# Filling TensorE's waits with unread products, changing banks and the order of three small steps in a transformer kernel

## The chip, the cores and the metric

The kernel runs on one core of one Trainium2 chip. The metric is the device time of one execution in microseconds (us). Shown is the median of several executions, and beside it one execution that the hardware profiler recorded. All times below are of that one core.

## What is computed

The reference runs two stacks over 256 tokens of width 1024. The first has 16 meta tokens in front (272 columns) and two layers. A layer norms its input, projects it by `w_in`, and feeds four branches: differential attention (a), gated linear attention in two directions (b), latent attention with rotary positions (c), windowed attention (d). Their outputs are projected, gated, summed (`merge`) and projected by `w_out`; then follows a feed-forward part with a convolution of width 3.

```
branches = jnp.stack([o_a, o_b, o_c, o_d], axis=2)
gates = jax.nn.sigmoid(gate_logits.reshape(bsz, T, N_BRANCH, D_MODEL))
merged = jnp.sum(jnp.einsum('btnw,nwd->btnd', branches, w_branch[l]) * gates, axis=2)
h = h + _rms_norm(merged @ w_out[l], norm_mix_post[l])
f = _conv_ffn(_rms_norm(h, norm_ffn_pre[l]), ffn_w_up[l], ...)
```

The second stack has two layers of swiglu, mixer, swiglu over 256 columns; the mixer is a convolution module in its first layer and pooling beside block attention (moba) in its second. A last norm ends it.

## The kernel before, in words

All weights come in slabs of 128 x 1024 numbers through a ring of six buffers (`ring`), in one fixed order, the list `STREAM` (644 slabs). A weight W is split into a rounded part `ring_hi` and a rest `ring_lo`; so is the input (`x_hi`, `x_lo`, or `z_hi`, `z_lo`, or `hid_hi`, `hid_lo`). A product with a slab is then three matmuls for each of eight (or six) blocks k, 24 in all: hi by hi (L403), hi by lo (L404), lo by hi (L405), all into one PSUM bank. `ring_hi` is written by ScalarE (ACT, L958) or, for a third of the `w_in` slabs, by VectorE (DVE, L1700); `ring_lo` by DVE (L1705) or, for some slabs, by GpSimd (POOL, L2488). `low_by(n)` says which.

Each engine has its own program, written out in order by hand, and engines wait for each other by semaphores. Before a bank is written again, TensorE (PE) waits for its last reader; that is `claim(b, *by)`, where `by` names the reader that the next claim will wait for. `begin(name)` waits until the slab's two halves are there. On ACT, `halves(slab)` makes the `ring_hi` of the slab three places further on in the stream, and that needs a free place among four (`HIGH`), so it waits until the slab before `slab` has been used by PE. `low_halves` is the same for `ring_lo` on DVE and POOL. The stream's DMAs are on SP's queue (L2741) and wait for the slab six places back.

Places that matter here:

- `slab_bank` (L289 and following): the bank of a slab. Most take the parity of their place in the stream; the slab (bk, l, 0) has bank 1 and so has (ak, l, 0), two places later. The slabs (mix, 0, 0..3) have banks 4 to 7, and (mix, 0, 4..7) banks 0, 1, 0, 1.
- `first_slab` (L408): the first slab of a part, whose input h is made at the same moment. For each k it has three matmuls (L416, L417, L419) and one of the float32 norm products with `ones` (L423). Its input is made by DVE (L1758, L1760: h; L1693: `z_lo`) and ACT (L997: `z_hi`).
- `norm_gathered` (L456): two norm products at the end of a part (L460, L462). ACT then makes the inverse root `std` (L978, L980).
- `mixers(l)` on PE (L639): among other things it ends with `gate(l, 1, 3)` (a gate is one dense slab), the rotary products (L500), `out_b` of unit 1 (two halves of 3 products of L581 and 8 small products of L586 each) and, for four heads, `scores_c` (L628, L629), gates and so on.
- `mix_out(layer)`: the projection of the second stack's mixer, eight slabs. DVE adds each to h (L1693, h <- bank); ACT makes `z_hi` (L997) and the square (L1485) of it and the next `ring_hi` (L958); DVE makes `z_lo` and the next `ring_lo` (L1705). On ACT the loop is `halves(mix j)`, then `square_x(j)`, which waits for DVE's h of slab j.
- ACT's and DVE's programs for the other parts are unchanged and appear only as the ones that are waited for.

Of the kernel before, what the change touches and what calls it, by code (L numbers as in the profile page):

```python
# [12 lines left out]
P = 128  # L13
KD = D_MODEL // P
# [152 lines left out]
def build(nc, d, out):  # L167
# [4 lines left out]
    with ctx:  # L172
# [13 lines left out]
        cst = sb("cst", N_CST)  # L186
# [104 lines left out]
        def slab_bank(name):  # L291
            if name[0] == "lat":
                return name[2]
            if name[0] in ("up", "gu"):
                n = 2 * name[2] + name[3]
                return n if name[2] < FZ else (n - 2 * FZ) % 4
            if name[0] == "bq" and name[2] == 0:
                return 6
            if name[0] in ("down", "down2"):
                return name[2] % 2  # L300
            if name[0:2] == ("mix", 0) and name[2] < 4:
                return 4 + name[2]
            return N[name] % 2

        def used(name):
# [61 lines left out]
        def tensor_program(pe, c):  # L367
# [3 lines left out]
            def claim(b, *by):  # L371
# [2 lines left out]
                read_by[b] = by  # L374
                return bank[b]

            def begin(name):
                n = N[name]
                assert n == count[0]
                count[0] += 1  # L380
                if STREAM[n][5]:
                    pe.wait_ge(*split(n))
                else:
                    pe.wait_ge(*loaded(n))
                return n % RING, n % HIGH

            def project_raw(name, x, cs, by, ready=None):
                i, _ = begin(name)
                b = claim(slab_bank(name), *by)
                for k in range(KD):  # L390
                    if ready:
                        pe.wait_ge(*at(*ready[k]))
                    m = pe.matmul(b[:, cs], ring[:, i, k * P:(k + 1) * P], x[:, k, cs], start=k == 0, stop=k == KD - 1)  # L393
                m.then_inc(sems["slab_used"], 1)
# [12 lines left out]

            def first_slab(name, b, cs, ready, norm_name, squares, ns):  # L408

                i, i_hi = begin(name)  # L410
                ps = claim(NB, act_, "log", *norm_name)
                for k in range(KD):
                    pe.wait_ge(*at(act_, "z_hi", *ready[k][2:]))
                    c0 = slice(k * P, (k + 1) * P)
                    x1, x2 = z_hi[:, k, cs], z_lo[:, k, cs]
                    pe.matmul(b[:, cs], ring_hi[:, i_hi, c0], x1, start=k == 0, stop=False)  # L416
                    pe.matmul(b[:, cs], ring_lo[:, i, c0], x1, start=False, stop=False)  # L417
                    pe.wait_ge(*at(*ready[k]))
                    m = pe.matmul(b[:, cs], ring_hi[:, i_hi, c0], x2, start=False, stop=k == KD - 1)  # L419
                    if k == KD - 1:  # L420
                        m.then_inc(sems["slab_used"], 1)
                    pe.wait_ge(*at(act_, *squares, k))
                    m = pe.matmul(ps[:, ns], ones, sq[:, k, ns], start=k == 0, stop=k == KD - 1)  # L423
                m.then_inc(*sig(pe_, "norm", *norm_name))
# [1 line left out]
            def project_z(name, cs, by):  # L426
                split_mm(name, claim(slab_bank(name), *by), z_hi, z_lo, 0, KD, cs, True, True)

            def project(name, cs, by, ready=()):
                split_mm(name, claim(slab_bank(name), *by), x_hi, x_lo, 0, KD, cs, True, True, ready)  # L430

            def project_tokens(name, by, tiles):
                i, i_hi = begin(name)
# [19 lines left out]
                    m = pe.matmul(ps[:, cs], ones, sq[:, k, cs], start=i == 0, stop=i == len(squares) - 1)  # L453
                m.then_inc(*sig(pe_, "norm", *name))

            def norm_gathered(name, last, cs=ALL):  # L456

                ps = claim(NB, act_, "log", *name)
                pe.wait_ge(*at(dve_, "gathered", *name))
                pe.matmul(ps[:, cs], ones, sq[:, 0, cs], start=True, stop=False)  # L460
                pe.wait_ge(*at(act_, *last))
                pe.matmul(ps[:, cs], ones, sq[:, KD - 1, cs], start=False, stop=True).then_inc(*sig(pe_, "norm", *name))  # L462
# [107 lines left out]
                                      v_b[r0:r0 + n, t, hh * P:(hh + 1) * P], start=True, stop=True)  # L570
                    m.then_inc(*sig(pe_, "ds", un, w, ch))

            def out_b(un):
                pe.wait_ge(*at(dve_, "state_read", un))
                for hh in range(2):
                    rr = slice(64 * hh, 64 * hh + 64)
                    b = claim(6 + hh, act_, "sqb", un, hh)
                    pe.wait_ge(*at(dve_, "masked", un, hh))
                    for i, t in enumerate((1, 2, 0)):
                        t0, n = TILES[t]  # L580
                        pe.matmul(b[:, t0:t0 + n], v_b[0:n, t, hh * P:(hh + 1) * P], att[0:n, hh, t0:t0 + n], start=i == 0,  # L581
                                  stop=False, skip_group_check=True)
                    todo = [(0, ch) for ch in (1, 2, 3, 4)] + [(1, ch) for ch in (0, 1, 2, 3)]
                    for i, (w, ch) in enumerate(todo):
                        a0, n = CHUNKS[ch][0:2]
                        m = pe.matmul(b[:, a0:a0 + n], state[rr, w, ch, :], q_dec[rr, w, a0:a0 + n], start=False,  # L586
                                      stop=i == len(todo) - 1, skip_group_check=True)
                    m.then_inc(*sig(pe_, "o", un, hh))
# [50 lines left out]
            def mixers(l):  # L639
# [88 lines left out]
                gate(l, 1, 2)  # L728
                latent_q(l, 0)
                latent_v(l, 0)  # L730
                gate(l, 1, 3)
                pe.wait_ge(*at(act_, "kpe", l))
                rope(("K", l), k_pe)
                rope_q(l, 0)
                out_b(B[1])
                for hd in range(4):
                    scores_c(l, hd)
                    first, second = gates_of(hd)
# [35 lines left out]
            def ffn(l):  # L774
                for j in range(KD):
                    b = claim(slab_bank(("out", l, j)), act_, "sqo", l, j)
                    split_mm(("out", l, j), b, z_hi, z_lo, 0, KD, kept(l), True, True,
                             [(dve_, "y_lo", l, k) for k in range(KD)] if j == 0 else ())
                norm_gathered(("out", l), ("sqo", l, KD - 1), kept(l))
                for j in range(NJ):  # L780
                    for gv in range(2):
                        name, by = ("up", l, j, gv), (dve_, "cv3", l, j, gv)
                        if j + gv == 0:
                            first_slab(name, claim(slab_bank(name), *by), kept(l), [(dve_, "z_lo", "ffn", l, k) for k in range(KD)],
                                       ("ffn", l), ("sqf", l), kept(l))
                        elif j < FZ:
                            project_z(name, kept(l), by)
                        else:
                            project(name, kept(l), by, [(dve_, "x_lo", l, k) for k in range(KD)] if (j, gv) == (FZ, 0) else ())
                for j in range(KD):  # L790
                    claim(slab_bank(("down", l, j, 0)), act_, "sqd", l, j)
                    for part, (k0, nk) in enumerate(DOWN):
                        project_down(("down", l, j, part), j, part, fed(l), [(pool_, "hid", l, k0 + k) for k in range(nk)] if j == 0 else ())
                norm_gathered(("down", l), ("sqd", l, KD - 1), fed(l))

            def swiglu(i):
                s = (0, 2, 3, 5)[i]
                for j in range(NJ):
                    for gv in range(2):
# [7 lines left out]
                        elif j < FZ:  # L807
                            project_z(name, SHIFTED, by)
                        else:
                            project(name, TEXT, by, [(dve_, "xs_lo", s, k) for k in range(KD)] if (j, gv) == (FZ, 0) else ())  # L810
                for j in range(KD):
                    claim(slab_bank(("down2", i, j, 0)), dve_, "xd", i, j)
                    for part, (k0, nk) in enumerate(DOWN):
# [15 lines left out]
            def mix_out(layer):  # L829
                whole = range(KD)  # L830
                if layer == 0:
                    for j in range(4):
                        begin(("mix", 0, j))
                        claim(slab_bank(("mix", 0, j)), dve_, "xm", 0, j)
                        mix_part(j, (4, 5, 6), True, False)
                    for j in range(4):
                        mix_part(j, (7,), False, False)
# [2 lines left out]
                    whole = range(4, KD)  # L840
                for j in whole:
                    b = claim(slab_bank(("mix", layer, j)), dve_, "xm", layer, j)
                    split_mm(("mix", layer, j), b, x_hi, x_lo, 0, KD, TEXT, True, True,
                             [(dve_, "y2_lo", layer, k) for k in range(KD)] if j == 0 else ())

# [12 lines left out]
            def conv_mixers():  # L858
# [1 line left out]
                first = [(act_, "xs", 1, k) for k in range(KD)]  # L860
                by = ("a", "a_gate", "cg", "bu", "bg")
                for n, (j, k) in enumerate(CONV_ORDER):
                    project_raw(("conv", j, k) if k < 4 else ("convg", j), u, TEXT, (act_, by[k], j), None if n else first)
                    if (j, k) in ((2, 1), (3, 0), (2, 2), (3, 2)):
                        centred({(2, 1): 0, (3, 0): 1, (2, 2): 2, (3, 2): 3}[j, k])
                    if (j, k) in ((1, 2), (1, 3), (2, 3), (3, 3)):
# [26 lines left out]
                t.then_inc(*sig(pe_, "pv", un, m))  # L893

            def moba():
                project(("moba", 0, 0), TEXT, (act_, "q", ("M", 0, 0)), [(dve_, "xs_lo", 4, k) for k in range(KD)])
                project(("moba", 0, 1), TEXT, (act_, "k", ("M", 0, 0)))
                for i in range(4):
                    project_tokens(("moba", i, 2), (act_, "v", ("M", 0, i)), QT2)
# [34 lines left out]
        def scalar_program(act, c):  # L934
# [598 lines left out]
            def mix_out(layer):  # L1533
# [3 lines left out]
                    for k in range(KD):  # L1537
                        mixed_high(layer, k, *((dve_, "pooled", k) if k < 4 else (act_, "o2", ("M", 0, k - 4), 1)))
                for j in range(KD):
                    if j:  # L1540
                        halves(("mix", layer, j))
                    if j == KD - 1:
                        log_exp_tables()
                    square_x(3 * layer + 2, j, dve_, "xm", layer, j)
# [1384 lines left out]
```

## Time and profile before

| | us |
|---|---|
| three executions | 2355.89, 2352.30, 2357.58 (median 2355.89) |
| the profiled execution, its own time | 2349.86 |
| its span, first to last instruction | 2348.1 |
| PE busy in the span | 2230.5 (95%) |
| DVE, ACT, POOL busy | 1509.0, 1121.0, 782.2 |

PE is busy nearly all the time, the others are not. An engine's "idle" time stands in brackets in the timeline, with the one that ended it. The clock column of the windows view is the share of full speed (2.4 GHz) that TensorE was granted: 1.00 or, in some stretches, 0.50.

### The profile page before, as it was taken

The numbers are of one execution on the slowest core, as the hardware profiler recorded it, in microseconds if no ns is written. First come the engines' busy times: TensorE is split into PE (matmuls) and PEld (weight loads), VectorE is DVE, ScalarE is ACT, GpSimd is POOL, SyncE is SP. The second block draws the span as 40 slices with busy tenths as digits, with TensorE's granted clock in tenths as the row PEclk, the third lists the DMA queues.
The fourth block names the chain that finished last, engine by engine and source line by source line (L and its number), as shares of the span: only waits on it lengthen the run. The fifth ranks groups of instructions, "written<-read, shape, count | busy, mean of one in ns | idle before, by whom it ended". The sixth has DMA issues, their size and how long they took to land.

```text
span 2348.1 us, 41898 instructions
## 1 busy us (share of the span) xinstructions
PE 2230.5 (95%) x16820; PEld 2081.1 (89%) x16820; DVE 1509.0 (64%) x2653; ACT 1121.0 (48%) x2056; POOL 782.2 (33%) x734
## 2 busy tenths in 40 slices
PE   7999999999999999999899999998999999998998
PEld 6878679889987787699799899988999999888998
DVE  5865579688777665797898664376644644436543
ACT  5554353565445553544655544424544543445443
POOL 3431223235525531232155143214332242231431
PEclk9999899999999997999999999999999999999999
DMA  7763358546775742577367555644556556544554
GB/s 237 199 194 104 117 205 297 188 147 213 255 227 154 213 137 79 191 284 260 121 214 248 192 180 180 188 141 130 170 189 180 178 183 184 170 135 135 184 181 130
DMA packets 121953, 429.38 MB, mean 183 GB/s; under 512 B 14960, under 2 KB 16928, under 8 KB 121633
## 3 DMA queue, kind: packets, MB, share of 16 engines
q1 hardware_dynamic: 94208, 333.80, 43.6%
q0 software_dynamic: 27408, 91.77, 13.1%
q8 instruction: 134, 2.20, 0.4%
q10 hardware_dynamic: 144, 1.13, 0.1%
q14 instruction: 59, 0.48, 0.1%
HBM read 425.55 MB, written 1.10 MB: 182 GB/s over the span
## 4 chain that ended last, share of the span: by engine, by line
PE 84%; DVE 8%; ACT 4%; issue 3%; POOL 1%; DMA 0%; SPq 0%; DVEq 0%; ACTq 0%; POOLq 0%
PE bank L403 21%; PE bank L405 21%; PE bank L404 21%; PE bank L393 3%; PE bank L492 2%; DVE ring_lo L1705 2%; PE bank L771 1%; PE bank L770 1%; PE bank L769 1%; ACT ring_hi L958 1%; PE bank L469 1%; PE bank L484 1%; PE bank L586 1%; PE bank L628 1%; PE bank L629 1%
## 5 line engine op out<-in xcount | busy, mean ns | idle before, releaser
L1705 DVE TENSOR_TENSOR ring_lo<-ring,ring_hi 128x1024 fp32r<-128x1024 f32 (+1 forms) x473 | 647.6, 1370 | 496.5 <-ACT ring_hi L958 496.3
L403 PE MATMUL bank<-x_hi,ring_hi 128*128 128x256 f32 (+2 forms) x3008 | 873.9, 291 | 33.3 <-issue 9.2
L404 PE MATMUL bank<-x_lo,ring_hi 128*128 128x256 f32 (+2 forms) x3008 | 864.4, 287 | 0.0
L405 PE MATMUL bank<-x_hi,ring_lo 128*128 128x256 f32 (+2 forms) x3008 | 863.3, 287 | 0.0
L958 ACT ACTIVATE ring_hi<-ring 128x1024 fp32r<-128x1024 f32 (+1 forms) x582 | 600.8, 1036 | 308.1 <-PE bank L405 239.7
L403 PEld LDWEIGHTS bank<-x_hi,ring_hi 128*128 128x128 f32 x3008 | 577.2, 192 | 54.4 <-issue 30.0
L405 PEld LDWEIGHTS bank<-x_hi,ring_lo 128*128 128x128 f32 x3008 | 578.0, 192 | 0.0
L404 PEld LDWEIGHTS bank<-x_lo,ring_hi 128*128 128x128 f32 x3008 | 575.9, 191 | 0.3
L2488 POOL TENSOR_TENSOR ring_lo<-ring,ring_hi 128x1024 fp32r<-128x1024 f32 (+1 forms) x151 | 384.4, 2546 | 564.7 <-ACT ring_hi L958 303.0
L405 PE MATMUL bank<-hid_hi,ring_lo 128*128 128x256 f32 (+1 forms) x1056 | 299.8, 284 | 0.0
L403 PE MATMUL bank<-hid_hi,ring_hi 128*128 128x256 f32 (+1 forms) x1056 | 298.6, 283 | 0.6 <-POOL ring_lo L2488 0.6
L404 PE MATMUL bank<-hid_lo,ring_hi 128*128 128x256 f32 (+1 forms) x1056 | 298.1, 282 | 0.0
L2623 POOL CAST hid_hi<-cv_sb 128x256 fp32r<-128x256 f32 (+1 forms) x132 | 96.5, 731 | 555.5 <-DVE cv_sb L2309 222.2
L403 PEld LDWEIGHTS bank<-hid_hi,ring_hi 128*128 128x128 f32 x1056 | 199.6, 189 | 0.8 <-issue 0.8
L404 PEld LDWEIGHTS bank<-hid_lo,ring_hi 128*128 128x128 f32 x1056 | 199.1, 189 | 0.0
L405 PEld LDWEIGHTS bank<-hid_hi,ring_lo 128*128 128x128 f32 x1056 | 199.0, 188 | 0.0
L1724 DVE CUSTOM_DVE_ANT_0 ada_ring<-ada_ring,cond 128x1024 f32<-128x1024 f32 x144 | 176.2, 1246 | 2.2 <-DMA ada_ring<-in_ada 2.2
L2500 POOL DMA_DIRECT2D ada_ring<-in_ada x144 | 82.2, 571 | 243.5 <-DVE mod L1724 235.9
L403 PE MATMUL bank<-z_hi,ring_hi 128*128 128x258 f32 (+1 forms) x472 | 139.0, 294 | 8.9 <-DVE z_lo L1693 7.1
L404 PE MATMUL bank<-z_lo,ring_hi 128*128 128x258 f32 (+1 forms) x472 | 135.8, 288 | 0.0
L405 PE MATMUL bank<-z_hi,ring_lo 128*128 128x258 f32 (+1 forms) x472 | 135.3, 287 | 0.0
L2625 POOL TENSOR_TENSOR hid_lo<-cv_sb,hid_hi 128x256 fp32r<-128x256 f32 (+1 forms) x132 | 102.0, 773 | 10.6
(336 smaller groups left out, 3048.6 us busy)
## 6 DMA issues: line engine op xcount, KB each, us to landing
ring<-in_w_gu SPq DMA_DIRECT2D x192, 512.0 KB, 3.5
ada_ring<-in_ada POOLq DMA_DIRECT2D x144, 512.0 KB, 5.1
ring<-in_w_in SPq DMA_DIRECT2D x136, 512.0 KB, 4.4
ring<-in_ffn_up SPq DMA_DIRECT2D x104, 512.0 KB, 3.5
ring<-in_w_down SPq DMA_DIRECT2D x64, 512.0 KB, 3.5
ring<-in_w_branch SPq DMA_DIRECT2D x32, 512.0 KB, 4.8
ring<-in_ffn_down SPq DMA_DIRECT2D x32, 512.0 KB, 4.7
ring<-in_w_down SPq DMA_DIRECT2D x32, 384.0 KB, 3.4
```

The costliest lines, as they stand in the source:

```text
L393: m = pe.matmul(b[:, cs], ring[:, i, k * P:(k + 1) * P], x[:, k, cs], start=k == 0, stop=k == KD - 1)
L403: pe.matmul(b[:, cs], ring_hi[:, i_hi, c0], x1, start=first and k == 0, stop=False)
L404: pe.matmul(b[:, cs], ring_hi[:, i_hi, c0], x2, start=False, stop=False)
L405: m = pe.matmul(b[:, cs], ring_lo[:, i, c0], x1, start=False, stop=last and k == nk - 1)
L492: m = pe.matmul(b[rows, 0:T], v[0:kn, kt, cols], pt_sb[0:kn, kt, :], start=kt == 0, stop=kt == 2)
L958: act.activation(ring_hi[:, n % HIGH, 0:cols], ring[:, i, 0:cols], ACT.Copy).then_inc(*sig(act_, "hi", n))
L1705: dve.tensor_tensor(ring_lo[:, i, 0:cols], ring[:, i, 0:cols], ring_hi[:, n % HIGH, 0:cols].bitcast(f32), ALU.subtract).then_inc(split(n)[ ...
L1724: dve.tensor_tensor_reduce(out=tile, in0=tile, in1=cond[:, :], scale=1.0, scalar=0.0, op0=ALU.mult, op1=ALU.add, accum_out=mod[:, l * ADA_ ...
L2488: pool.tensor_tensor(ring_lo[:, i, 0:cols], ring[:, i, 0:cols], ring_hi[:, n % HIGH, 0:cols].bitcast(f32), ALU.subtract).then_inc(split(n) ...
L2500: pool.dma_start(ada_ring[:, t % ADA_RING, :], d["ada"][l * ADA_TILES + k]).then_inc(sems[f"ada_loaded{t % ADA_RING}"], 16)
L2623: pool.tensor_copy(hid_hi[:, j, cs], at_j[:, cs]).then_inc(*sig(pool_, "hid_hi", *name))
L2625: pool.tensor_tensor(hid_lo[:, j, cs], at_j[:, cs], hid_hi[:, j, cs].bitcast(f32), ALU.subtract).then_inc(*sig(pool_, *name))
```

## The change

A function `unread(b, n)` on PE issues n float32 products of the constants `ones` and `cst` (128 x 256) into bank b. Nobody reads them; the slab that follows starts the bank anew. Counted over the program there are 69 of them: 5 ahead of each of five `first_slab`, 4 ahead of the first `out` slab of both layers, 3 ahead of slab (up, l, 3, 0) of both layers and of (gu, i, 3, 0) of the four swiglus, 4 in `norm_gathered` of the second layer's `down`, 3 ahead of (mix, 0, 3), 2 ahead of (mix, 1, 0), 4 ahead of the first `conv` slab, 5 ahead of the first `moba` slab. (The condition `j == 4 and low_by(...) == pool_` holds for no slab: the POOL slab there is (up, l, 5, 1).)

Two bank tables change: (ak, l, 0) takes bank 3, and (mix, 0, j) takes bank (j + 4) % 8, so eight different ones. On PE, `gate(l, 1, 3)` moves from ahead of the rotary products to between the two halves of `out_b`. On ACT, the loop of `mix_out` calls `halves` for slab j + 1 ahead of `square_x(j)` and no more for slab j.

```diff
+            if name[0] == "ak" and name[2] == 0:
+                return 3
-            if name[0:2] == ("mix", 0) and name[2] < 4:
-                return 4 + name[2]
+            if name[0:2] == ("mix", 0):
+                return (name[2] + 4) % 8
...
+            def unread(b, n):
+                for _ in range(n):
+                    pe.matmul(b[:, 0:2 * P], ones, cst[:, 0:2 * P], start=True, stop=True)
...
             def first_slab(name, b, cs, ready, norm_name, squares, ns):
+                unread(b, 5)
                 i, i_hi = begin(name)
...
-            def project(name, cs, by, ready=()):
-                split_mm(name, claim(slab_bank(name), *by), x_hi, x_lo, 0, KD, cs, True, True, ready)
+            def project(name, cs, by, ready=(), idle=0):
+                b = claim(slab_bank(name), *by)
+                unread(b, idle)
+                split_mm(name, b, x_hi, x_lo, 0, KD, cs, True, True, ready)
...
-            def norm_gathered(name, last, cs=ALL):
+            def norm_gathered(name, last, cs=ALL, idle=0):
                 ps = claim(NB, act_, "log", *name)
+                unread(ps, idle)
                 pe.wait_ge(*at(dve_, "gathered", *name))
...
-            def out_b(un):
-                pe.wait_ge(*at(dve_, "state_read", un))
-                for hh in range(2):
+            def out_b(un, halves=(0, 1)):
+                if 0 in halves:
+                    pe.wait_ge(*at(dve_, "state_read", un))
+                for hh in halves:
...
-                gate(l, 1, 3)
                 pe.wait_ge(*at(act_, "kpe", l))
                 rope(("K", l), k_pe)
                 rope_q(l, 0)
-                out_b(B[1])
+                out_b(B[1], (0,))
+                gate(l, 1, 3)
+                out_b(B[1], (1,))
...
+                    unread(b, 0 if j else 4)
...
-                            project(name, kept(l), by, [(dve_, "x_lo", l, k) for k in range(KD)] if (j, gv) == (FZ, 0) else ())
+                            project(name, kept(l), by, [(dve_, "x_lo", l, k) for k in range(KD)] if (j, gv) == (FZ, 0) else (),
+                                    3 if (j, gv) == (FZ, 0) or j == 4 and low_by(N[name]) == pool_ else 0)
...
-                norm_gathered(("down", l), ("sqd", l, KD - 1), fed(l))
+                norm_gathered(("down", l), ("sqd", l, KD - 1), fed(l), 4 * l)
...
+                        b = claim(slab_bank(("mix", 0, j)), dve_, "xm", 0, j)
+                        unread(b, 3 if low_by(N["mix", 0, j]) == pool_ else 0)
                         begin(("mix", 0, j))
-                        claim(slab_bank(("mix", 0, j)), dve_, "xm", 0, j)
...
+                    unread(b, 2 if layer > 0 and j == 0 else 0)
...
                 for j in range(KD):
-                    if j:
-                        halves(("mix", layer, j))
+                    if j < KD - 1:
+                        halves(("mix", layer, j + 1))
                     if j == KD - 1:
                         log_exp_tables()
                     square_x(3 * layer + 2, j, dve_, "xm", layer, j)
```

## Rows read from the trace of the kernel before

**Rows 1.** The page's first part: busy time of PE and its weight loads.
```profile
PE 2230.5 (95%) x16820; PEld 2081.1 (89%) x16820; DVE 1509.0 (64%) x2653; ACT 1121.0 (48%) x2056; POOL 782.2 (33%) x734
```

**Rows 2.** Span and mean granted TensorE clock of the core.
```profile
core 0: 2348.1 us, clock 0.978
```

**Rows 3.** Windows; columns: PE, PEld, DVE, ACT, POOL busy, clock, DMA share, GB/s.
```profile
257.10:270.60 13.50, 13.50 (x43) 8.79 (x42) 4.72 (x8) 2.18 (x8) 2.54 (x1) 0.50 0.00 1
461.90:465.20 3.30, 2.94 (x9) 2.58 (x10) 3.20 (x9) 2.50 (x7) 0.00 (x0) 0.50 0.00 0
919.30:936.20 16.90, 16.90 (x57) 11.81 (x57) 7.17 (x10) 3.81 (x11) 3.45 (x3) 0.50 0.07 20
1096.80:1100.00 3.20, 3.20 (x17) 3.20 (x17) 0.84 (x1) 1.70 (x3) 0.00 (x0) 0.50 0.40 116
2117.40:2120.60 3.20, 2.69 (x12) 2.72 (x13) 2.71 (x9) 1.41 (x5) 0.00 (x0) 0.50 0.00 0
```

**Rows 4.** Waits of PE: total us, times, longest.
```profile
PE bank L416 <- ACT z_hi L997: 10.5, 4, 2.7
PE bank L403 <- ACT k_b L1003: 5.9, 2, 3.2
PE bank L403 <- POOL ring_lo L2488: 5.8, 5, 2.1
```

**Rows 5.** Timeline of DVE and PE in the first mix_out: start, duration.
```profile
1632.61 1.23 DVE L1705 TENSOR_TENSOR ring_lo<-ring,ring_hi 128x1024 fp32r<-128x1024 f32 x1 [1.10 <-ACT ring_hi L958]
...
1634.29 0.58 PE L403 MATMUL bank<-x_hi,ring_hi 128*128 128x256 f32 x1 [4.15 <-DVE h L1693]
...
1636.06 1.22 DVE L1705 TENSOR_TENSOR ring_lo<-ring,ring_hi 128x1024 fp32r<-128x1024 f32 x1 [1.10 <-ACT ring_hi L958]
...
1644.11 0.48 DVE L1693 SCALAR_TENSOR_TENSOR h<-bank,mod,h 128x256 f32<-128x256 f32 x1
```

**Rows 6.** Timeline of PE and DVE in the second mix_out.
```profile
2121.74 0.28 PE L403 MATMUL bank<-x_hi,ring_hi 128*128 128x256 f32 x1
...
2124.58 0.28 PE L403 MATMUL bank<-x_hi,ring_hi 128*128 128x256 f32 x1
...
2145.33 0.48 DVE L1693 SCALAR_TENSOR_TENSOR h<-bank,mod,h 128x256 f32<-128x256 f32 x1
```

**Rows 7.** Timeline of PE: scores of head 0 and head 1, first layer.
```profile
259.76 1.09 PE L628 MATMUL bank<-k_c,q_c 128*16 128x272 f32 x2
...
266.61 0.59 PE L403 MATMUL bank<-x_hi,ring_hi 128*128 128x272 f32 x1
...
282.44 0.63 PE L628 MATMUL bank<-k_c,q_c 128*16 128x272 f32 x2
...
286.18 0.39 PE L403 MATMUL bank<-x_hi,ring_hi 128*128 128x272 f32 x1
```

**Rows 8.** Timeline of ACT behind the slabs bk and ak, both layers.
```profile
48.36 0.38 ACT L1003 ACTIVATE k_b<-bank 128x272 f32<-128x272 f32 x1
...
53.64 0.40 ACT L1003 ACTIVATE k_a<-bank 128x272 f32<-128x272 f32 x1
...
717.76 0.40 ACT L1003 ACTIVATE k_a<-bank 128x272 f32<-128x272 f32 x1 [2.05 <-PE bank L405]
```

**Rows 9.** Timeline of DVE beside a first_slab (first layer's up).
```profile
462.31 0.49 DVE L1693 SCALAR_TENSOR_TENSOR z_lo<-h,prm,z_hi 128x272 fp32r<-128x272 f32 x1
...
463.55 0.50 DVE L1693 SCALAR_TENSOR_TENSOR z_lo<-h,prm,z_hi 128x272 fp32r<-128x272 f32 x1
```

**Rows 10.** The chain that ended last: one convolution slab, eight float32 products (two instructions each).
```profile
1571.46 3.45 PE bank L393 x16
```

**Rows 11.** Timeline of PE in the very first first_slab, early and late.
```profile
17.83 0.82 PE L416 MATMUL bank<-z_hi,ring_hi 128*128 128x272 f32 x1
...
22.10 0.49 PE L416 MATMUL bank<-z_hi,ring_hi 128*128 128x272 f32 x1
```

**Rows 12.** Timeline of PE at slab (up, 0, 3, 0).
```profile
487.37 0.37 PE L403 MATMUL bank<-x_hi,ring_hi 128*128 128x272 f32 x1 [0.35 <-issue]
```

More of the change, by code:

```diff
@@ L385, in begin, with project_raw @@
                 return n % RING, n % HIGH
-            def project_raw(name, x, cs, by, ready=None):
+            def project_raw(name, x, cs, by, ready=None, idle=0):
                 i, _ = begin(name)
                 b = claim(slab_bank(name), *by)
+                unread(b, idle)
                 for k in range(KD):
@@ L427, in project_z @@
                 split_mm(name, claim(slab_bank(name), *by), z_hi, z_lo, 0, KD, cs, True, True)
-            def project(name, cs, by, ready=()):
-                split_mm(name, claim(slab_bank(name), *by), x_hi, x_lo, 0, KD, cs, True, True, ready)
+            def project(name, cs, by, ready=(), idle=0):
+                b = claim(slab_bank(name), *by)
+                unread(b, idle)
+                split_mm(name, b, x_hi, x_lo, 0, KD, cs, True, True, ready)
             def project_tokens(name, by, tiles):
@@ L809, in swiglu @@
                         else:
-                            project(name, TEXT, by, [(dve_, "xs_lo", s, k) for k in range(KD)] if (j, gv) == (FZ, 0) else ())
+                            project(name, TEXT, by, [(dve_, "xs_lo", s, k) for k in range(KD)] if (j, gv) == (FZ, 0) else (),
+                                    3 if (j, gv) == (FZ, 0) else 0)
                 for j in range(KD):
@@ L862, in conv_mixers @@
                 for n, (j, k) in enumerate(CONV_ORDER):
-                    project_raw(("conv", j, k) if k < 4 else ("convg", j), u, TEXT, (act_, by[k], j), None if n else first)
+                    project_raw(("conv", j, k) if k < 4 else ("convg", j), u, TEXT, (act_, by[k], j), None if n else first, 0 if n else 4)
                     if (j, k) in ((2, 1), (3, 0), (2, 2), (3, 2)):
@@ L895, in moba @@
             def moba():
-                project(("moba", 0, 0), TEXT, (act_, "q", ("M", 0, 0)), [(dve_, "xs_lo", 4, k) for k in range(KD)])
+                project(("moba", 0, 0), TEXT, (act_, "q", ("M", 0, 0)), [(dve_, "xs_lo", 4, k) for k in range(KD)], 5)
                 project(("moba", 0, 1), TEXT, (act_, "k", ("M", 0, 0)))
```

## The prediction

> **What bounds the kernel now.** I read the page's busy times first: PE works 95% of the span [rows 1]. So time can only come from PE's idle moments, from PE work done at half clock, or from PE being late for a chain that ends on another engine. The granted clock comes next: its mean is 0.978 [rows 2]. Stretches at half clock lose half their length, so 0.022 x 2348.1 = 51.7 us of full-speed time are missing, in 18 stretches (one is the very end, where PE has nothing left). Then PE's waits, to see what each gap waits for [rows 4], and the timelines at the places of the edits, to see what is late next. The sum is made against the profiled execution (2349.86, of it 1.8 outside the span); the median of the runs is 6.0 above it, and I carry the difference over unchanged.
>
> **The moved gate.** The two largest stretches at half clock, 13.5 and 16.9 us [rows 3], begin where the small products of out_b follow one another and last until a dense gate slab has run. PE is 100% busy in both. If they went, the ceiling is half of 30.4 = 15.2 us. The rows of the scores give a finer share: six products took 266.61 - 259.76 = 6.85 us at half clock, and 286.18 - 282.44 = 3.74 at full [rows 7], so 45% is saved rather than 50%: 13.8. The gate (24 dense matmuls, about 3 us) now stands between the halves, so no run of small products is longer than one half of out_b plus the two rotary products. That run still exists, and a short fall (3.3 us at half clock, as the stretch at 461.9 [rows 3]) may remain in each layer: 2 x 1.65 = 3.3. I take 13.8 - 3.3 = 10.5; ends 0 (the clock falls all the same) and 15.2. What the gate covered before: PE now reaches the rotary products and out_b 3 us earlier. The states were finished about 10 us before out_b, the latent query's copies some 4, so I cost the lost cover at 0. Behind it ACT waits 3 us longer for the gate before its out_b copies, which nobody needs until two heads later; and SP's ring place is freed late by two half units in a stretch where the DMA share is near 0 [rows 3].
>
> The Trainium skill ("TensorE: Matmul & The Clock Gate", "HAM oscillation") gives as its rule that there be no long idle gaps of PE. The next section of the same page, "A second HAM failure mode", says that many micro-idles between groups also make the clock swing. The trace speaks for the second: the clock fell at 257.1 with PE counted busy throughout. By the first rule alone the moved gate, which closes no gap, brings nothing; that is a rival below.
>
> **The first attention's key.** Slab ak waited for ACT's copy of k_b, 5.9 us in two waits [rows 4]. Bank 3 frees it. What is late next is the copy k_a, in ACT's order. In layer 0 it ran at 53.64 and ACT was busy up to it with work that waits for no part of ak [rows 8]; PE gains about 2.6 us of head start, but the softmax behind it is made by ACT and DVE, of which one 1.1 us wait goes: 1.0. In layer 1 k_a waited 2.05 us for PE [rows 8], and this is what the ACT chain gains: 2.0. Together 3.0; ends 0 and 5.9 + 5 of half-clock work.
>
> **The first mix_out.** Here PE is not the bound. ring_lo follows ring_lo at 1636.06 - 1632.61 = 3.45 us [rows 5], while a slab takes PE 2124.58 - 2121.74 = 2.84 [rows 6]. The loop is: DVE adds h (0.48), ACT makes z_hi, the square and only then ring_hi, DVE makes ring_lo after waiting 1.10 for it [rows 5], and adds the next h. With `halves` ahead of the square, ring_hi starts as soon as PE has used the slab, and that 1.10 leaves DVE's turn: about 2.35 us, less than PE's 2.84. Followed slab by slab, DVE's last h comes at about 1635.5 rather than 1644.11 [rows 5]: 8.6, of which 0.3 returns as ACT's table load ahead of the last z_hi. The norm and the root behind it shift alike: 8.3. The wait of 4.15 us at 1634.29 for bank 0 [rows 5] is a symptom of the same lag; with new banks alone DVE's loop would still take 3.45 a slab. So nearly all of the 8.3 belongs to the `halves` line, and I give the banks 0 to 1. Ends 4 and 9.5.
>
> **The second mix_out.** The same loop. PE sends a slab each 2.84, so the last slab ends at about 2142.0 and DVE's h could follow at 2142.3 rather than 2145.33 [rows 6]: 3.0, of which 0.3 is lost because the slab after it then takes its full time: 2.7. Two unread products in the gap ahead may keep the clock in the stretch at 2117.4; PE would then save about 1.4 on its first slab. One in two: 0.7. Together 3.4; ends 1 and 4.5.
>
> **The unread products.** One costs 3.45 / 8 = 0.43 us at full clock [rows 10], 69 cost 29.7. Nearly all stand in gaps: five (2.15) in the waits for z_hi, 10.5 us in four [rows 4]; three (1.29) in gaps near 2.3 at the swiglus; three in a POOL wait of 2.1 [rows 4] in the first mix_out. What does the kept clock give there? Look at the first stretch, 461.9 to 465.2 [rows 3]: DVE's z_lo come each 463.55 - 462.31 = 1.24 us [rows 9], and PE needs 3 x 2.84 / 24 + 0.43 = 0.79 a block at full clock [rows 6, 10] and 1.6 at half. PE falls behind by about 1 us in the first three blocks and has caught up before the last block. So in the first_slab stretches the clock costs nothing, and keeping it brings nothing: 0 for 20 of the 25 (0 to 0.5 each). The other five stand at the very start, where the matmuls have the length of half clock, 0.82 against 0.49 later [rows 11], until about 21.5 us, with their input ready; a faster rise gives the first root 0 to 2.6, and POOL's ring_lo takes part back: 1.0. At the `out` slabs PE is the bound: the stretch at 1096.8 [rows 3] gives 1.6. At moba and conv 0.3. At (up, l, 3, 0) three products meet a gap of 0.35 [rows 12] and make the slab 0.9 late. The slabs behind it wait for DVE's ring_lo, which doesn't wait for this one, so most is taken up: 0 a layer, 0.9 as the bad end; I take 0.5 for both. No product stands ahead of the long POOL waits at (up, l, 5, 1).
>
> The Trainium skill ("TensorE: Matmul & The Clock Gate", "What happens when you issue a matmul") says that matmuls stay in program order, only weight loads are drawn ahead. By that rule every product longer than its gap delays the real slab by the excess, which is how I cost the place above.
>
> **Sum.** 10.5 + 3.0 + 8.3 + 3.4 + 1.0 + 1.6 + 0.3 - 0.5 = 27.6 us. From 2349.9 that is 2322.3 for a profiled run, and from the median 2355.9 it is 2328.3; I say 2328. A difference under 0.2% (4.7 us) can't be told from none.
>
> **Rivals.**
> - *The clock falls at out_b as before* (the first rule of the page above). For: rotary products, their wait and one half are 5 us of small work. Against: in the unit before, two halves in a row with dense slabs around them keep clock 1.00. It gives 27.6 - 10.5 = 17.1, so 2339. Chance 0.2.
> - *mix_out stays bound by DVE.* ring_lo and h share DVE, and if ring_hi on ACT came late again for another reason (the z_hi of the slab before), the period would stay near 3.2 rather than under 2.84. Then 8.3 + 2.7 shrink to about 3: 2336. Chance 0.1.
> - *Everything holds the clock*: no short falls remain, and the two of 3.3 us at unchanged places in the mixers go too by another phase: 2328 - 6 = 2322 or below. Chance 0.1.
> - *Slower: the products overrun.* Place: all 69 on PE's in-order queue. Price: 0.43 each at full clock and 0.86 at half. If the clock is low when they run, five take 4.3 in a gap of 2.7, three take 2.6 in 2.3. Over 21 places that is up to 59 - 33 (the gaps) = 26 us, and it decides once less than a fifth of it is taken up by DVE's pace and the moved gate fails as well: 2361. Against: they come right behind dense slabs, at full clock. Chance 0.03.
> - *The edits do less than they say*: both the clock and the loops stay. Then only ak is left: 2352. Chance 0.03.
> - My forecast: 0.54.
>
> **Numbers.** The forecast 2328 with its ends (ak, mix_out, the phase of the falls, each some 3 to 4 us) covers 2318 to 2336; the first two rivals carry it to 2343. Range 2317 to 2343. Faster by over 0.2%: 0.94; within: 0.03; slower: 0.03.
>
> **What would show it.** Right: mean clock near 0.987; no stretch at half clock over 7 us in the two out_b places; ring_lo in the first mix_out at PE's pace of about 2.85 us and its last h some 8 us closer to its first; the wait for k_b gone, k_a unchanged in layer 0; 138 more PE instructions. Wrong: the long stretches still there at 0.50; DVE's 1.10 waits for ring_hi still in mix_out; new waits of PE behind the products, that is real slabs that start later than their inputs.

## The result and the profile after

Over four executions each, the changed kernel's median is 2328.65 us (2325.97 to 2332.31), the kernel before has 2356.36 (2352.30 to 2357.58). The ratio is 0.9891, with a 95% interval of 0.9871 to 0.9911: faster by 27.7 us by the medians, by 25.7 by the ratio. The forecast was 2328. The profiled execution took 2325.97, against 2349.86: 23.9 less.

The page's busy times and the clock, after:

```profile
PE 2243.2 (97%) x16958; PEld 2091.9 (90%) x16958; DVE 1510.2 (65%) x2653; ACT 1121.3 (48%) x2056; POOL 783.1 (34%) x734
```
```profile
core 0: 2324.2 us, clock 0.988
```

PE has 138 more instructions (69 products of two each, [rows 1]) and is busy 12.7 us longer in a shorter span. The mean clock rose by 0.010 [rows 2].

Waits of PE after (total us, times, longest):

```profile
PE bank L411 <- DVE ring_lo L1724: 8.0, 7, 1.9
PE bank L411 <- POOL ring_lo L2507: 6.1, 6, 2.6
PE bank L487 <- DVE small L1751: 2.4, 1, 2.4
...
PE bank L425 <- ACT z_hi L1016: 1.8, 4, 0.5
```

The wait for `k_b` is gone from the list and the one for `z_hi` fell from 10.5 to 1.8 [rows 4]. The second doesn't mean that 8.7 us were won: the products now fill that time, and the real matmuls begin no earlier. One wait is new, 2.4 us for `small`.

Windows of four places, from the same instruction to the same instruction in both kernels: the two `out_b` stretches of layers 0 and 1, the first and the second `mix_out`. Columns as in [rows 3]. After:

```profile
242.11:267.23 25.12, 23.93 (x125) 18.33 (x125) 9.10 (x17) 6.37 (x19) 2.99 (x2) 0.86 0.19 56
906.56:929.79 23.23, 22.05 (x125) 16.46 (x125) 10.40 (x17) 6.34 (x19) 3.47 (x3) 0.93 0.19 60
1605.00:1645.44 40.44, 39.37 (x320) 38.58 (x320) 31.68 (x65) 26.30 (x43) 1.38 (x2) 1.00 0.55 175
2095.76:2141.89 46.13, 44.81 (x355) 43.04 (x355) 34.00 (x70) 29.00 (x51) 5.52 (x4) 1.00 0.51 155
```

Before:

```profile
244.08:272.30 28.22, 27.02 (x125) 19.15 (x125) 10.93 (x17) 6.47 (x19) 4.35 (x3) 0.76 0.16 50
908.38:937.77 29.39, 28.21 (x125) 20.20 (x125) 11.81 (x22) 6.44 (x19) 4.43 (x4) 0.71 0.18 53
1615.78:1664.26 48.48, 41.13 (x314) 40.10 (x314) 32.19 (x65) 26.09 (x43) 1.38 (x2) 0.93 0.47 148
2115.40:2165.80 50.40, 45.60 (x345) 44.28 (x345) 34.12 (x70) 28.86 (x51) 5.50 (x4) 0.93 0.44 138
```

Two kinds of gain can be told apart here. At `out_b` PE has the same 125 instructions and simply needs less time for them: 27.02 to 23.93 and 28.21 to 22.05, with the clock column up from 0.76 to 0.86 and from 0.71 to 0.93. That is 3.1 and 6.2 us. In the first `mix_out` PE's busy time falls by only 1.8 us while the stretch shortens by 8.0: there mostly waiting went. The second `mix_out` gives 4.3. (The busy times after hold the unread products of these stretches: 6 and 10 more instructions.)

Timeline of the first `mix_out` after, DVE and PE, and below it the first `h` of before:

```profile
1609.15 0.48 DVE L1712 SCALAR_TENSOR_TENSOR h<-bank,mod,h 128x256 f32<-128x256 f32 x1 [2.29 <-PE bank L842]
...
1616.41 0.28 PE L411 MATMUL bank<-x_hi,ring_hi 128*128 128x256 f32 x1
...
1616.75 1.22 DVE L1724 TENSOR_TENSOR ring_lo<-ring,ring_hi 128x1024 fp32r<-128x1024 f32 x1
...
1619.01 1.21 DVE L1724 TENSOR_TENSOR ring_lo<-ring,ring_hi 128x1024 fp32r<-128x1024 f32 x1
...
1619.25 0.28 PE L411 MATMUL bank<-x_hi,ring_hi 128*128 128x256 f32 x1
...
1624.78 0.49 DVE L1712 SCALAR_TENSOR_TENSOR h<-bank,mod,h 128x256 f32<-128x256 f32 x1
```
```profile
1619.94 0.48 DVE L1693 SCALAR_TENSOR_TENSOR h<-bank,mod,h 128x256 f32<-128x256 f32 x1 [2.29 <-PE bank L825]
```

DVE's `ring_lo` have no bracket any more: nothing is waited for. They come each 2.26 us instead of 3.45 [rows 5], and PE starts a slab each 2.84, with no wait between. From the first `h` to the last are 1624.78 - 1609.15 = 15.6 us; before, from 1619.94 to 1644.11 (the last `h` of [rows 5]), 24.2. The 2.26 is DVE's own turn: it begins behind PE and catches up, and its last `h` comes right behind PE's last slab. PE, with no wait between its slabs, now sets when the stretch ends.

The key of the first attention after: ACT's copies `k_b` and `k_a` in layer 0, and the new wait of PE in layer 1:

```profile
48.13 0.38 ACT L1022 ACTIVATE k_b<-bank 128x272 f32<-128x272 f32 x1
...
53.21 0.38 ACT L1022 ACTIVATE k_a<-bank 128x272 f32<-128x272 f32 x1
...
718.73 0.49 PE L487 MATMUL bank<-cst,v_t 128*16 128x128 f32 x3 [2.37 <-DVE small L1751]
```

In layer 0 the copy came 0.4 us earlier than at 53.64 [rows 8], though PE had been made free by some 2.6 us. Of the 0.4, 0.2 had come already ahead of `k_b` (48.13 against 48.36), so the edit's own share is 0.2. In layer 1 the whole stretch is 2.2 shorter, and the time that PE gained beyond this it spends waiting for DVE's `small`.

The places add up as 3.1 + 6.2 + 8.0 + 4.3 + 0.2 + 2.2 = 24.0. Outside them 5.7 more went: 1.7 ahead of 189 us, 1.8 at the second layer's `out` slabs, 1.3 behind 1167 us, 0.9 at moba. What went ahead of 189 us can't be put down to the products at the start: in the profile of experiment 1, which changes nothing there, 1.4 went as well. The kernel before has a fall of the clock at 49 us, and experiment 1's profile has none there. Against this, 4.7 us came in the second layer's mixer ahead of `out_b` (840 to 908 us), where no edit stands, and about 1 in small pieces. In the first layer's mixer 3.0 went between 189 and 210 us and 3.0 came back ahead of `out_b`, also without an edit. The falls of the clock from 840 us on:

```profile
849.00:854.00 5.00, 5.00 (x26) 4.55 (x25) 3.06 (x8) 2.77 (x7) 0.00 (x0) 0.66 0.00 0
863.00:871.00 8.00, 8.00 (x35) 7.21 (x36) 6.54 (x17) 5.48 (x12) 0.00 (x0) 0.57 0.00 0
877.00:884.00 7.00, 7.00 (x32) 6.88 (x33) 2.11 (x6) 2.59 (x8) 0.26 (x1) 0.51 0.00 1
```

Before, this stretch had two short ones, at 881 to 886 and 895 to 899 us. PE counts as busy throughout. So falls appeared where nothing was changed (the same three stand in the profiles of experiments 6 and 9, not in that of 10), and the experiments had to show how much of any difference is of that kind.

### The profile page after: what moved, and what is told of

It is laid out like the page before. It is cut to its first block, busy times and chain, and to the rows that moved or that the text cites. A ratio compares the mean times of both kernels' runs of the same rounds, so it can differ in the third digit from the quotient of the medians.

```text
span 2324.2 us, 42168 instructions
## 1 busy us (share of the span) xinstructions
PE 2243.2 (97%) x16958; PEld 2091.9 (90%) x16958; DVE 1510.2 (65%) x2653; ACT 1121.3 (48%) x2056; POOL 783.1 (34%) x734
## 4 chain that ended last, share of the span: by engine, by line
PE 84%; DVE 8%; ACT 4%; issue 2%; POOL 1%; DMA 0%; DVEq 0%; ACTq 0%; POOLq 0%
PE bank L411 21%; PE bank L413 21%; PE bank L412 21%; PE bank L401 3%; PE bank L504 2%; DVE ring_lo L1724 2%; PE bank L785 1%; PE bank L784 1%; PE bank L783 1%; PE bank L481 1%; PE bank L496 1%; ACT ring_hi L977 1%; DVE u L1712 1%; PE bank L599 1%; DVE x_lo L1712 1%
## 5 line engine op out<-in xcount | busy, mean ns | idle before, releaser
L2644 POOL TENSOR_TENSOR hid_lo<-cv_sb,hid_hi 128x256 fp32r<-128x256 f32 (+1 forms) x132 | 102.2, 774 | 10.6
```

The source lines that it names most:

```text
L2644: pool.tensor_tensor(hid_lo[:, j, cs], at_j[:, cs], hid_hi[:, j, cs].bitcast(f32), ALU.subtract).then_inc(*sig(pool_, *name))
```

## The experiments

Each kernel ran in five rounds against the kernel before on the same chip. Line numbers in fences are those of the kernel shown. All ratios are to the kernel before as it ran beside the same experiments (1 to 4, 5 to 8, 9 to 12); the us given as a gain are the ratio's distance from 1 times 2355, and the difference of the medians may stand up to some 3 us from it.

**1. ACT's order alone.** The kernel before with only

```diff
-                    if j:
-                        halves(("mix", layer, j))
+                    if j < KD - 1:
+                        halves(("mix", layer, j + 1))
```

> The kernel before with the changed order of halves in ACT's mix_out and nothing else. My theory: this line alone breaks the DVE loop of 3.45 us a slab. The stretch from PE's POOL wait in the first mix_out to the first x_hi slab of the swiglu behind it (48.5 us before, 40.4 after the whole change) gets to 41 to 42, and the one from the pooled products of the second mix_out to the same place behind it (50.4 before, 46.1 after) to 47 to 48. In all 10 to 11 us faster than before. Rival (the banks carry it: PE waited 4.15 us for bank 0): the first stretch stays over 46, and the whole is under 5 us faster.

Median 2344.11 against 2353.93; ratio 0.9953 (0.9936 to 0.9971): 11.1 us. Its DVE in the first `mix_out`, and the windows of the first and the second `mix_out`:

```profile
1632.36 1.22 DVE L1705 TENSOR_TENSOR ring_lo<-ring,ring_hi 128x1024 fp32r<-128x1024 f32 x1
1634.62 1.22 DVE L1705 TENSOR_TENSOR ring_lo<-ring,ring_hi 128x1024 fp32r<-128x1024 f32 x1
```
```profile
1616.78:1658.83 42.05, 39.63 (x314) 39.17 (x314) 31.74 (x65) 26.44 (x43) 1.38 (x2) 0.96 0.56 169
2112.14:2158.35 46.21, 42.44 (x345) 41.45 (x345) 34.03 (x70) 28.99 (x51) 5.49 (x4) 1.00 0.51 157
```

The same 2.26 as in the whole change, with the old banks. What I put at 8.3 + 2.7 = 11.0 is all there; the second stretch is shorter than expected, 46.2 against 47 to 48.

**2. The banks of the first `mix_out` alone.**

```diff
-            if name[0:2] == ("mix", 0) and name[2] < 4:
-                return 4 + name[2]
+            if name[0:2] == ("mix", 0):
+                return (name[2] + 4) % 8
```

> The kernel before with banks (j + 4) % 8 for the slabs of the first mix_out and nothing else. My theory: DVE's last h stays at its time, since DVE and ACT still take 3.45 us a slab; the 4.15 us wait of PE for bank 0 goes away but turns up as waits for ring_lo; the stretch of 48.5 us shrinks by 0 to 1, the whole by 0 to 1. Rival (the banks carry it): the stretch shrinks by 4 to 8 us.

2356.68 against 2353.93; ratio 1.0007 (0.9995 to 1.0019): nothing. DVE's timeline and the first of PE's waits over the whole program (7.1 before):

```profile
1634.10 1.23 DVE L1705 TENSOR_TENSOR ring_lo<-ring,ring_hi 128x1024 fp32r<-128x1024 f32 x1 [1.11 <-ACT ring_hi L958]
...
1637.56 1.23 DVE L1705 TENSOR_TENSOR ring_lo<-ring,ring_hi 128x1024 fp32r<-128x1024 f32 x1 [1.11 <-ACT ring_hi L958]
```
```profile
PE bank L403 <- DVE z_lo L1693: 12.0, 5, 2.8
```

The period is still 3.45 and the 1.10 wait is still there. PE no longer waits 4.15 for a bank; it waits as long in sum, in other places, put down to other instructions of DVE. The wait for the bank was the lag's symptom. Nor do the banks bring anything once the order is changed: the first `mix_out` takes 42.05 us in experiment 1 with the old ones and 42.01 in experiment 6 with the new, each with a fall at its start.

**3. The moved gate alone.**

```diff
-                gate(l, 1, 3)
                 pe.wait_ge(*at(act_, "kpe", l))
                 rope(("K", l), k_pe)
                 rope_q(l, 0)
-                out_b(B[1])
+                out_b(B[1], (0,))
+                gate(l, 1, 3)
+                out_b(B[1], (1,))
```

> The kernel before with the gate moved between the halves of out_b and nothing else. My theory: the stretch from the latent query of head 0 to that of head 1 (28.2 and 29.4 us before, 25.1 and 23.2 after the whole change) gets to 22 to 26 us in both layers, about 10 us faster in all. Rival (the clock falls all the same, only idle gaps matter): both stay within 1 us of before.

2346.54 against 2353.93; ratio 0.9955 (0.9937 to 0.9974): 10.6 us. But its eleven executions lie between 2335.41 and 2353.67, and their mean clocks between 0.983 and 0.976. The profiled one, 2347.59, still falls twice in layer 1:

```profile
909.00:917.00 8.00, 8.00 (x41) 7.73 (x40) 2.81 (x3) 0.96 (x3) 3.07 (x2) 0.57 0.21 55
919.00:930.00 11.00, 10.98 (x35) 7.31 (x34) 5.88 (x13) 2.75 (x9) 1.38 (x2) 0.53 0.06 13
```

Its two stretches at `out_b`, layers 0 and 1:

```profile
243.93:265.96 22.03, 20.83 (x125) 15.29 (x125) 9.13 (x17) 6.39 (x19) 3.02 (x2) 1.00 0.20 64
901.23:930.57 29.34, 28.16 (x125) 21.07 (x125) 11.83 (x22) 6.35 (x19) 4.45 (x4) 0.71 0.20 61
```

I had expected 22 to 26 in both. Layer 0 has it, with no fall at all; layer 1 has gained nothing against 29.39. The edit takes away the certainty of the long fall, not the fall. All the profiles together show how far. In the seven profiles with the gate in its old place these stretches take 28.2 to 29.7 and 29.4 us. In the seven with the moved gate (the changed kernel was profiled twice, here and in experiment 9) layer 0 takes 22.0 once, 25.1 five times and 29.7 once (experiment 12); layer 1 takes 23.2 once, 24.8 three times (experiments 10 to 12) and 29.3 three times (3, 6 and 9). In the mean that is 4.2 + 2.9 = 7.1 us.

**4. The products alone.** The changed kernel with the other four edits undone.

> The kernel before with the 69 unread products and nothing else. My theory: beside first_slab, DVE is the bound, so a kept clock gives nothing there; the products give some 1 us at the start, 1.6 at the second layer's out slabs, 0.7 at the second mix_out, in all 2 to 4 us. Rival A (each stretch at half clock that goes gives back half its length): 1.7 us for each of six to eight stretches, 10 to 14 us. Rival B (products overrun their gaps): slower by 3 us or more.

2344.43 against 2353.93; ratio 0.9961 (0.9947 to 0.9975): 9.2 us, where I had 3.1. A miss, and the only large one.

**5. Bank 3 for the slab ak alone.**

```diff
+            if name[0] == "ak" and name[2] == 0:
+                return 3
```

> The kernel before with bank 3 for (ak, l, 0) and nothing else. My theory: the wait for k_b goes, but ACT's copy k_a and the softmax behind it come next: 1 us in the first layer, 2 in the second, 3 us in all. Rival: the two waits (5.9 us) and the half-clock work behind them (2 to 5 us) all come off: 8 to 11 us.

2351.83 against 2353.33; ratio 0.9995 (0.9983 to 1.0007), which can't be told from nothing. In its profile the stretch of layer 1 is 2.2 us shorter, and in layer 0 `k_a` follows `k_b` 0.2 sooner, just as in the whole change. So the edit's worth is read from the profile, 2.4 us, and a single median doesn't resolve it.

**6. The whole change without the products.** `unread` with `range(0)`.

> The changed kernel without the 69 unread products (banks, order of halves and moved gate stay). New theory, after the kernel with only the products was 9 us faster: the clock falls behind a gap of over 2 us in some executions and not in others, and the products take these falls away at places where PE is the bound; the profiled execution of before had hardly any of them there. Then this kernel is 6 to 10 us slower than the whole change, 17 to 21 us faster than before, and its profile has falls behind the gaps at the out slabs or the swiglus' fourth pair. My old theory: 3 us slower than the whole change, 24 us faster than before.

2338.22 (2330.21 to 2347.78) against 2353.33; ratio 0.9929 (0.9905 to 0.9954): 16.7 us, against 25.7 and 28.3 (experiment 9) for the whole: the products are worth 9 to 12 here too, though the intervals leave some 7 us to either side. Rows of its windows:

```profile
1098.00:1102.00 4.00, 4.00 (x23) 4.00 (x22) 1.23 (x1) 1.69 (x3) 0.00 (x0) 0.57 0.42 131
1361.00:1365.00 4.00, 4.00 (x24) 4.00 (x23) 2.51 (x5) 2.33 (x4) 2.05 (x2) 0.57 0.01 4
1617.00:1621.00 4.00, 3.72 (x19) 3.75 (x20) 2.02 (x7) 0.00 (x0) 0.13 (x1) 0.57 0.00 0
...
2112.00:2116.00 4.00, 3.91 (x20) 3.94 (x21) 2.29 (x7) 1.00 (x4) 0.00 (x0) 0.57 0.00 0
```

These are falls at dense slabs: at the second layer's `out`, in a swiglu behind the gap ahead of its slab (gu, i, 3, 0), in the first and ahead of the second `mix_out`. The changed kernel has none at these places in its first profile. In the profiled execution of before the ones in the swiglu and at the start of the first `mix_out` are absent as well, though the gap in the swiglu is there (the timeline of PE, before):

```profile
1360.30 0.36 PE L403 MATMUL bank<-x_hi,ring_hi 128*128 128x256 f32 x1 [2.27 <-issue]
```

The other two, at the `out` slab and the second `mix_out`, it does have [rows 3]. The fourteen profiles settle what this means, read at places ahead of which products stand that aren't in `first_slab`; there are 44 such products. At the second layer's `out` slab and at moba all seven profiles without the 44 have a fall, before's too. At six more places before's profile has none: three swiglu slabs (1360, 1664 and 1856 us on its clock), the first `conv` slab (1535), the start of the first `mix_out` (1616) and the last swiglu (2166). The other six profiles without the 44 have 3, 3, 1, 3, 5 and 4 falls there, 19 in all. The seven with them have none at any of the six, and one at the `out` slab (experiment 11).

**7 and 8. The products split.** Seven has only the 25 ahead of `first_slab`, eight only the other 44; nothing else is changed.

```diff
             def first_slab(name, b, cs, ready, norm_name, squares, ns):
 
+                unread(b, 5)
                 i, i_hi = begin(name)
```

> The kernel before with only the 25 unread products ahead of first_slab. Theory: beside first_slab DVE is the bound and the kept clock gives nothing but the quicker start: 0 to 2 us faster than before, though the stretches at half clock behind 461, 680, 1124 and 1333 us are gone. Rival: each stretch that goes gives 1.7 us, 6 to 8 us.

> The kernel before with the 44 unread products that don't stand ahead of first_slab. Theory: here PE is the bound behind the gaps, so nearly all of the 9 us of the 69 products is here: 6 to 9 us faster than before. Rival: half or less of it, under 4.

Seven: 2353.78 against 2353.33; ratio 1.0000 (0.9987 to 1.0013). Eight: 2344.29; ratio 0.9964 (0.9947 to 0.9980), 8.5 us. In seven's profile the falls of before behind these slabs (such as that at 461.9 [rows 3]) are gone, and its twelve executions have a mean clock of 0.9795 against 0.9765. 0.003 of 2353 is 7 us of full-speed work kept, and not one of them shows in the time. So the gain of the products is made by the 44, within the 3 us that seven's interval leaves to either side.

**9. The whole change once more**, on the same chip as 10 to 12.

> The changed kernel again, as the measure for the three kernels beside it: 24 to 29 us faster than the kernel before.

2323.68 (2319.41 to 2336.13) against 2355.35; ratio 0.9880 (0.9857 to 0.9903): 28.3 us. The profiler had hit the slowest of the six:

```profile
915.00:923.00 8.00, 8.00 (x42) 7.74 (x40) 2.92 (x3) 0.96 (x3) 3.07 (x2) 0.57 0.14 43
925.00:936.00 11.00, 11.00 (x36) 7.22 (x34) 5.88 (x13) 2.87 (x9) 1.29 (x2) 0.53 0.03 10
```

This is the same program as the one profiled first, with the same 0.57 and 0.53 as in experiment 3 at a place where the other execution had one fall of some 3.3 us (23.23 us at a mean clock of 0.93). The six executions in order of mean clock: 0.985 took 2336.13, 0.986 2333.55, 0.990 2322.41 and 2324.96, 0.991 2321.65, 0.993 2319.41. A difference of 0.008 is 18.7 us of full-speed work, and the time differs by 16.7.

**10. Twice the products**, 138.

> The changed kernel with 138 unread products, twice as many at each place. If they stand in gaps of PE and the rest is DVE's pace, they cost only what exceeds the gap: 4.3 us into gaps of 2.6 ahead of first_slab is taken up by DVE (0 to 1 us each of five); 2.6 into gaps of 2.3 at the swiglus costs 0.5 each; 3.4 into 2.2 at conv and out costs 1.2 each of three; (up, 3, 0) 1.3 to 2 each; in all 5 to 10 us slower than the changed kernel. If every product counts: 30 us slower.

2327.20; ratio 0.9898 (0.9875 to 0.9920), 3.5 us above experiment 9 with overlapping intervals, where I had expected 5 to 10. The granted clock is the best of all profiles:

```profile
core 0: 2323.5 us, clock 0.994
```

The next two were tries for something better still.

**11 and 12. One more dense slab between halves, and products at (up, l, 4, 1) and (up, l, 5, 1).** Twelve has both, eleven the first:

```diff
-                out_b(B[0])
+                out_b(B[0], (0,))
                 project(("bv", l, 2), ALL, (act_, "vt", B[1], 0))
+                out_b(B[0], (1,))
```

> The changed kernel with the slab (bv, l, 2) moved between the two halves of the first unit's out_b as well. The clock falls in most profiles somewhere in this stretch (214 to 232 us, 863 to 880 us). If a dense slab between small products is what helped at the second unit, 1 to 4 us faster than the changed kernel; if the falls come from the other small products around it (turned keys, inner scores), no difference.

> As the kernel with both units split, and with three unread products ahead of (up, l, 4, 1) and two ahead of the POOL slab (up, l, 5, 1), where the changed kernel has waits of 1.8 and up to 2.6 us and a fall right behind (494, 1150 us). If PE is the bound behind them, 1.5 us a layer faster than the split alone; if DVE's ring_lo is (my view: DVE is busy without a break there), no difference, or a few tenths slower.

Eleven: 2323.39 (2316.75 to 2327.00); ratio 0.9866 (0.9848 to 0.9883). Twelve: 2324.73; ratio 0.9874 (0.9855 to 0.9892). Both intervals overlap that of experiment 9, and eleven's median is 0.3 us below it. Neither is shown to be better.

## Why the prediction was right, and where not

The time came out as forecast. The steps, one by one:

- **First and second `mix_out`, 8.3 and 3.4.** Measured in the profile 8.0 and 4.3; the order on ACT alone gave 11.1 by the ratio where the two places had 8.3 + 2.7. Experiments 1 and 2 show the mechanism: the order carries it, the banks nothing that can be measured. From first to last, DVE's `h` took 8.5 us less (8.6 forecast). The 8.0 hides one thing: with the order alone the first stretch takes 42.0, and the last 1.6 down to 40.4 are a fall at its start that the products take away and that before's profile didn't have. The rival that DVE stays the bound is refuted by DVE's missing waits. One sign was put loosely: `ring_lo` came at DVE's own turn of 2.26 (I had said 2.35) and not at PE's 2.84, since DVE starts behind and catches up.
- **The moved gate, 10.5.** Measured 9.3 in the profiled pair, 10.6 alone (6 to 15 by the interval) and 7.1 in the mean of the profiles. The size is about right, the picture was not: I took a short fall in each layer for certain. The traces show from no fall up to two falls that together cost as much as the long one, and which comes differs between executions of one program (the changed kernel's first profile and that of experiment 9). The rival that the clock falls all the same is thus true of some executions, and the sign of no stretch at half clock over 7 us holds in the first profile and not in experiment 9's, where one lasts some 10 (11.00 us at 0.53). As to the rule of the Trainium skill ("TensorE: Matmul & The Clock Gate", "HAM oscillation"), by which the moved gate would bring nothing as it closes no gap: it brought 7 to 10 us without closing one, so long gaps can't be the only cause. Whether the section on micro-idles that follows it on that page names the cause isn't shown: from 250.87 us to the fall at 257.1 PE was idle once, for 0.62.
- **The key, 3.0.** Measured 2.2 in layer 1 (2.0 forecast) and 0.2 in layer 0 (1.0 forecast). "One 1.1 us wait goes" fails in layer 0.
- **The `out` slabs, 1.6.** Measured 1.8.
- **What failed: the unread products, in all 1.0 + 1.6 + 0.7 + 0.3 - 0.5 = 3.1.** Alone they gave 9.2, and 9 to 12 on top of the others. "In the first_slab stretches the clock costs nothing" held: 25 products, 0 us, within 3. That leaves the 1.0 for a quicker start neither shown nor refuted. The step that failed is the one that priced the other 44, "Two unread products ... one in two: 0.7", "at moba and conv 0.3", and nothing at all for the swiglus and the first `mix_out`. I listed the falls of one execution and let the products take away only these. The six other profiles without the 44 have 19 falls at six places where that execution did not (experiment 6), each for some 1.5 us where PE is the bound: experiment 6 loses 1.5 behind 1361 and 1.6 behind 1617. That is about 3 falls or 5 us an execution, an estimate from these rows, beside the 2.1 that I had for the 44; they gave 8.5. With that the sentence "the median of the runs is 6.0 above it, and I carry the difference over unchanged" fails too. The 24 executions of before beside experiments 1 to 4 show the difference to be clock: 0.970 took 2364.49, 0.978 took 2348.07 to 2352.79. The change took part of it away.
- **Why the total still fits.** The single edits measured 11.1 + 10.6 + 9.2 + 1.2 - 1.6 (banks) = 30.5 by their ratios; the whole 25.7 and 28.3. By edit, the forecast's 27.6 were 11.0, 10.5, 3.1, 3.0 and 0. So the products were put 6 too low, the key and the banks together 3 too high, and the sum of the singles exceeds the whole by 2 to 5 us, which the intervals (some 3 to 5 us to each side) allow. The profiled execution took 2325.97, 3.7 more than the 2322.3 forecast for it, and the median lies only 2.7 above it rather than 6.0: the two misses cancel. The total was right partly by luck.
- **Overrun.** The rival that the products delay real slabs has its price in experiment 10: 69 more cost some 4 us (3.5 by the medians, 4.2 by the ratios), if anything, net of what their higher clock gave. At 0.43 each [rows 10] they are 29.7 us of work, so most of it still finds gaps, and the gap of 0.35 at (up, l, 3, 0) was rightly put at little: in layer 0 PE ran 0.7 us late at that slab and had it back 10 us later.

What stays open: the mean worth of the moved gate to better than some 3 us, since its executions spread over 18; and what decides, from one execution to the next, whether a given gap or run of small products brings a fall. That experiment 10 is slower than 9 was not resolved.

## What to carry to other kernels

A profile shows the clock's falls of one execution. Before pricing an edit that keeps TensorE busy, compare the profiled execution's mean clock with that of the other executions, profile more than one if you can, and count every gap ahead of dense work at which TensorE is the bound as a place where a fall may come, whether or not the trace has one; at places bound by another engine a kept clock is worth nothing. And where a helper engine serves both a chain and the weights of later slabs, look at what it does while it waits for the chain: one line moved ahead of that wait was worth as much as any other edit here.

## What was not expected of the hardware

- The falls move between executions of one program: six executions of the changed kernel had mean clocks from 0.985 to 0.993, and the time went with them (16.7 us for 18.7 us of full-speed work). In the two sets of 24 executions of before the correlation of time and clock was -0.93 and -0.95.
- Clock isn't time: the products ahead of `first_slab` raised the mean clock by 0.003 at no gain, the doubled ones raised the mean over executions from 0.989 to 0.992 at no gain.
- A gap of 2.3 us ahead of a dense slab had a fall behind it in three of the seven profiles without products there (1361 us in experiment 6) and none in the profiled execution of before, with the same gap.
